# Attention of a two-layer hybrid block: where the second maximum, the second copy and the spread of the inverse sums stand in each pair of heads

## The reference

```python
def softmax_attend(q, k, v, sink):
    s = jnp.einsum('bqgrd,bkgd->bgrqk', q, k).astype(jnp.float32) * (q.shape[-1] ** -0.5)
    if sink is None:
        p = jax.nn.softmax(s, axis=-1)
    else:
        ...
        p = jax.nn.softmax(jnp.concatenate([sk, s], axis=-1), axis=-1)[..., 1:]
    return jnp.einsum('bgrqk,bkgd->bqgrd', p.astype(v.dtype), v)
...
outs.append(blocked_attend(q, jnp.concatenate([k, kc], axis=1), jnp.concatenate([v, vc], axis=1)))
```

## Time and profile before

| | |
|---|---|
| time, median of 3 runs (lowest, highest) | 2471.43 us (2469.43, 2474.56) |
| the profiled execution | 2481.41 us, span 2479.6 us |
| TensorE busy | 2265.1 us, 91% of the span |
| VectorE, ScalarE, GpSimd busy | 986.8, 678.8, 767.7 us (40%, 27%, 31%) |
| mean granted clock of TensorE | 0.946 of full |
| chain that ended last | PE 79%, DVE 12%, ACT 5% |

### The profile page before, as it was taken

How to read it: one execution, slowest core, us unless ns; L and a number is a source line. 1 busy time by engine, 2 the same in 40 slices (tenths; PEclk the granted TensorE clock), 3 DMA queues, 4 the chain that set the end, 5 groups by cost and what they waited for, 6 DMA issues and landing times.

```text
span 2479.6 us, 46004 instructions
## 1 busy us (share of the span) xinstructions
PE 2265.1 (91%) x19396; PEld 1817.8 (73%) x19396; DVE 986.8 (40%) x1477; ACT 678.8 (27%) x1181; POOL 767.7 (31%) x546
## 2 busy tenths in 40 slices
PE   5999888889989799999999899988888988999997
PEld 3888565558868488888888668846657866788886
DVE  3000555554670741414232330055556664632443
ACT  3001355641321320211111221135562222221221
POOL 2332243003213123232232244124303214444443
PEclk9999999977999899999999989899987999999998
DMA  6122000030011212212113222200030013232331
GB/s 251 54 65 108 35 1 0 6 119 3 4 53 51 94 60 65 62 59 68 59 59 134 74 80 98 79 34 1 0 117 9 4 55 125 89 98 93 94 101 59
DMA packets 45404, 162.42 MB, mean 66 GB/s; under 512 B 5504, under 2 KB 5504, under 8 KB 45024
## 3 DMA queue, kind: packets, MB, share of 16 engines
q1 hardware_dynamic: 44480, 157.89, 19.0%
q0 software_dynamic: 800, 2.69, 0.3%
HBM read 158.46 MB, written 2.10 MB: 65 GB/s over the span
## 4 chain that ended last, share of the span: by engine, by line
PE 79%; DVE 12%; ACT 5%; issue 2%; POOL 1%; DMA 0%; SPq 0%; POOLq 0%; DVEq 0%; ACTq 0%
PE ps L1364 76%; PE ps L1639 2%; DVE part_h L1014 1%; DVE small L1117 1%; DVE hT L1007 1%; DVE xT L1032 1%; DVE flat L1348 1%; ACT flat L772 1%; DVE ps L1114 1%; DVE flat L1030 1%; ACT flat L754 1%; POOL flat L527 1%; PE ps L1901 0%; DVE flat L1097 0%; ACT flat L704 0%
## 5 line engine op out<-in xcount | busy, mean ns | idle before, releaser
L1364 PE MATMUL ps<-part_hi,wparts 128*128 128x512 f32 (+1 forms) x3072 | 815.0, 353 | 28.1 <-DVE part_h L1014 10.0
L1364 PEld LDWEIGHTS ps<-part_hi,wparts 128*128 128x128 f32 x3072 | 544.9, 191 | 117.0 <-DVE part_h L1014 15.5
L508 POOL TENSOR_TENSOR wparts<-flat,wparts 128x1024 fp32r<-128x1024 f32 x184 | 447.5, 2432 | 535.1 <-ACT wparts L930 529.3
L1364 PE MATMUL ps<-flat 64*64 64x32 f32 (+8 forms) x8812 | 497.8, 266 | 68.5 <-ACT flat L772 30.3
L1364 PEld LDWEIGHTS ps<-flat 64*64 64x64 f32 (+4 forms) x8812 | 385.0, 148 | 166.7 <-issue 75.1
L1364 PE MATMUL ps<-part_h,wparts 128*128 128x512 f32 (+1 forms) x1344 | 473.8, 353 | 0.0
L1364 PE MATMUL ps<-part_mlp,wparts 128*128 128x512 f32 (+1 forms) x1536 | 417.5, 359 | 14.6 <-DVE part_h L1014 9.9
L1364 PE MATMUL ps<-part_lo,wparts 128*128 128x512 f32 x960 | 341.8, 356 | 0.0
L1364 PEld LDWEIGHTS ps<-part_mlp,wparts 128*128 128x128 f32 x1536 | 275.5, 191 | 61.9 <-DVE part_h L1014 11.6
L930 ACT ACTIVATE wparts<-flat 128x1024 fp32r<-128x1024 f32 x112 | 118.8, 1061 | 704.2 <-PE ps L1364 704.2
L1364 PEld LDWEIGHTS ps<-part_h,wparts 128*128 128x128 f32 x1344 | 257.5, 192 | 32.2 <-issue 0.2
(11 more groups left out here) (201 smaller groups left out, 1994.8 us busy)
## 6 DMA issues: line engine op xcount, KB each, us to landing
flat<-w_dram SPq DMA_DIRECT2D x128, 512.0 KB, 3.6
flat<-wmod_dram SPq DMA_DIRECT2D x88, 512.0 KB, 5.4
flat<-win_dram SPq DMA_DIRECT2D x40, 512.0 KB, 3.6
flat<-wout_dram SPq DMA_DIRECT2D x16, 512.0 KB, 3.7
hT<-wmod_dram SPq DMA_DIRECT2D x8, 512.0 KB, 7.7
xT<-xT_dram SPq DMA_DIRECT2D x8, 384.0 KB, 6.5
flat<-rope_dram SPq DMA_DIRECT2D x2, 1024.0 KB, 5.6
out_dram<-xT SPq DMA_DIRECT2D x8, 256.0 KB, 2.0
```

The costliest lines, as they stand in the source:

```text
L508: pool.tensor_tensor(wlo[q % 2], src, whi[q % 2], ALU.subtract).then_inc(s_used[q], 1)
L1364: return pe.matmul(out, lhsT, rhs, start=start, stop=stop)
```

## The change

It has four parts, all inside the loop over the pairs.

1. TensorE: `turns(2p + 1)` stands before `spread_sums(p)`. The spread no longer waits for `s_on` of the last pair, and `output` waits for `s_on` of the last pair instead of `s_spre`.
2. The spread's result has a PSUM bank of its own (bank 7) instead of a quarter of the product's bank 6.
3. ScalarE: the copy to `over_sum` stands behind the second `turned`, and waits for `s_on` of the last pair as well as for `s_spr`. In passes 1 and 2 `exps(2p + 2)` stands ahead of the second `turned`.
4. VectorE: in passes 1 and 2 both maxima stand ahead of the second `turned`; in the other passes it stays between them.

```diff
-        O_AT, SPREAD_AT = 3072, 3072 + P
+        O_AT, SPREAD_AT = 3072, 3584
...
                         for p in range(6):
+
+                            def exps_of(h):
+                                exps(h % 12, at + (12 if h >= 12 else 0))
+
                             turned(2 * p)
+                            if p in (1, 2):
+                                exps_of(2 * p + 2)
+                            turned(2 * p + 1)
                             act.wait_ge(s_spr, i * 6 + (turned0 // 2 + p + 1))
+                            act.wait_ge(s_on, 1 + i * 6 + (turned0 // 2 + p))
                             nc_.activation(over_sum, ps[:, SPREAD_AT:SPREAD_AT + P], ACT.Copy).then_inc(s_spre, 1)
-                            turned(2 * p + 1)
-                            for h in (2 * p + 2, 2 * p + 3):
-                                exps(h % 12, at + (12 if h >= 12 else 0))
+                            if p not in (1, 2):
+                                exps_of(2 * p + 2)
+                            exps_of(2 * p + 3)
...
                             for h in (2 * p + 2, 2 * p + 3):
-                                if h % 2:
+                                if h % 2 and p not in (1, 2):
                                     turned(2 * p + 1)
                                 peak(h % 12, at + (12 if h >= 12 else 0), i)
+                            if p in (1, 2):
+                                turned(2 * p + 1)
                             normed(p)
...
                             pe.wait_ge(s_sum, pairs + (p + 1))
-                            pe.wait_ge(s_on, 1 + pairs + p)
                             for g in range(2):
...
                             pe.wait_ge(s_pta, 1 + done + (2 * p + 2))
                             pe.wait_ge(s_ptd, 1 + done + (2 * p + 2))
-                            pe.wait_ge(s_spre, pairs + (p + 1))
+                            pe.wait_ge(s_on, 1 + pairs + p)
...
                             scores((p + 1) % 6, at + (2 * p + 2), i + (asked + (1 if p == 5 else 0)))
+                            turns(2 * p + 1)
                             spread_sums(p)
-                            turns(2 * p + 1)
                             output(p)
```

## The result

The changed kernel takes 2457.16 us (median of 5 runs, 2455.93 to 2458.88); the kernel before, beside it, 2474.56 us (2469.43 to 2480.43). The ratio is 0.9921 with a 95% interval of 0.9898 to 0.9945: between 14 and 25 us faster. The median moved by 17.4 us, the forecast was 12.2 us, to a time of 2459.2. The profiled execution went from 2481.41 us (span 2479.6) to 2458.63 us (span 2456.8), 22.8 us.

A forecast was written before the change was run, and what follows sets the result against it. Wide blocks were taken as bound mostly by TensorE plus one hand-over with ScalarE in each pair. Wide blocks 11.2 plus narrow 1.0 made 12.2 us, off the median 2471.43: 2459.2 us, range 2453 to 2467.

The forecast's parts named there:

- The spread leaves the path: Wide pairs: spread behind the second transposes hides in the wait for ScalarE's copy; product 0.37 us earlier, 0.36 taken.
- Passes 1 and 2: Wide blocks, low-rank scores: product comes earlier though both maxima precede VectorE's copy; saved 0.33 to 0.37, 0.36 us taken.
- Passes 3 and 4: Wide blocks, window scores: product waits for VectorE's chain, which starts at the scores in both programs; saved 0.
- Wide blocks: Eight attention blocks: four of six pairs save 0.36, 1.44 us a block, 1.26 in each layer's last; 11.2 together.
- Narrow blocks: Two blocks of layer 0, ScalarE nearly full: 0.50 us saved a block, 1.0 in all; bounds -3.4 to +4.4.
- The loss in pass 4: Narrow blocks, pair 4: second transposes may not start before ScalarE's first copy; exponential at 488.47 instead of 488.19, 0.28 lost.
- the step that gave 0: Narrow blocks, pair 3: ScalarE's exponentials start where they did, so 0 is saved.
- TensorE's clock: Rival, first narrow block's half clock: fall gone saves 4.1 us more (2455), one more gives 2463; gains beyond forecast 0.06.

The follow-up runs named there:

- the pair with the matmuls: Kernel before and changed kernel, each with three unread 512-column identity matmuls behind the narrow blocks' first scores: 2473.75 and 2458.47 us.
- the changed kernel's second trace: The changed kernel timed and profiled again without edit, beside the kernel before: 2457.01 us, ratio 0.9919.
- ScalarE's part alone: Kernel before with ScalarE's copy of the sums behind its second copy and a bank of its own, spread left in place: 2482.52 us, ratio 1.0014.
- TensorE's part alone: Kernel before with the spread behind the second transposes and its own bank, ScalarE's copy of the sums left in front: 2478.85 us, ratio 1.0014.
- the kernel before with its three matmuls: Kernel before plus three unread 512-column identity matmuls behind the narrow blocks' first scores: 2473.75 us, ratio 0.9964.

## Why the prediction was right, and where it was off

*Direction, size and range were right*, and so was the mechanism. That the time came out 2.0 us from the forecast is in part luck. The forecast was taken off the median of three runs, 2471.43 us, which is close to what the kernel before takes at its better clock (2472.9), where the changed kernel always was. Off the medians measured later (2474.56 to 2482.87) the same 12.2 us would have given 2462 to 2471 us, partly outside the range. Read by its own steps:

- **The spread leaves the path (0.37 a pass).** Right in passes 0 and 5 of the wide blocks. Idle time in front of the product fell from 0.69 to 0.32, and the spread issued twice fits in the same gap. What makes it free is the wait for ScalarE's copy, as the prediction said.
- **It is only free together with ScalarE's move.** The prediction priced the parts together and didn't say this. Each alone gave nothing (ratio 1.0014 both times).
- **Passes 1 and 2: taken 0.36, came 0.42 and 0.43.** The step compared two possible starts of the product and took the later one by ScalarE, 0.92 + 0.64 behind the scores' end. Behind the low-rank scores ScalarE's copy started only 0.77 behind the scores' end (1689.42 to 1690.19, see pass 1 above), and then VectorE's copy is the last one. The prediction's own figure by VectorE, 1709.34 against 1709.74 before, gives 0.40. The term was 16 x 0.07 = 1 us too small.
- **Passes 3 and 4: nothing, right.** From first transposes to first transposes they take 5.85 and 5.50 us, before and after.
- **Wide blocks, 1.44 a block, measured 1.59**: over eight, with the two last ones 0.2 less, 12.3 instead of 11.2 us.
- **Narrow blocks, 0.50 a block, 1.0 in all, measured 1.3.** At a clock of 1.00 in both traces (the pair with the matmuls) the first block is 0.53 shorter, 17.77 to 17.24 us from its first transposes to those of the second block. The second is 1.06 shorter up to the work behind its last product (17.77 to 16.71 us in the first profiles), but only 0.77 up to the tanh, since the last exponential stands behind the copy of the sums there. By pass the second block came as 0.22, 0.32, 0.32, 0.19, -0.21 and 0.22, where 0.18, 0.23, 0.23, 0, -0.28 and 0.14 were taken. The first block's passes 0 and 5 gained nothing (-0.03 and -0.05), since the transposes of the next pass wait for an exponential there. The row of the wait behind pass 5, in the first profile, and the rows of pass 4 of the second block:

```profile
465.56 0.41 PE L1649 MATMUL ps<-kf,flat 128*128 128x128 f32 x2 [0.30 <-ACT flat L754]
...
477.50 0.26 ACT L772 ACTIVATE flat<-ps 128x128 f32<-128x128 f32 x1
...
477.86 0.41 PE L1649 MATMUL ps<-kf,flat 128*128 128x128 f32 x2 [0.20 <-issue]
...
478.31 0.28 ACT L772 ACTIVATE flat<-ps 128x128 f32<-128x128 f32 x1 [0.55 <-PE ps L1649]
```

  The loss in pass 4 was foretold, and for this reason: ScalarE's first copy ends at 477.76, the second transposes start behind it at 477.86, the second copy is at 478.31, and both exponentials come later. The other terms were mis-sized by up to 0.1. In pass 3 the step that gave 0 was wrong by 0.19. ScalarE's exponentials did start where they did (2.03 us into the pass, 2.02 before), but the next transposes had not waited for them: they followed the product, which now comes 0.21 sooner.
- **TensorE's clock was a rival for one fall more or less, 4.1 us. It was more than that.** Passes 0 to 2 of the narrow blocks after, as the earlier trace rows:

```profile
446.20:456.60 10.40, 10.03 (x60) 6.58 (x60) 4.90 (x17) 5.85 (x24) 0.00 (x0) 0.67 0.00 1
465.56:473.68 8.12, 7.40 (x60) 4.82 (x60) 4.86 (x18) 5.85 (x25) 0.00 (x0) 1.00 0.00 0
```

  10.40 and 8.12 us instead of 13.05 and 8.98: the first block lost 2.3 us to the clock instead of 4.1. But filling the wait takes 9 us (5 to 13) off the kernel before, and nothing that could be measured off the changed one. So of the 17 to 21 us between the medians 14 to 15 are the order (12.2 forecast), and the rest is clock that the kernel before loses in more of its executions: its mean granted clock is under 0.949 in 48 of 73, that of the changed kernel in none of 13.
- **Behind the attention.** The first two profiles differ by 22.8 us, of which the attention has 15.7. The rest lies almost wholly between layer 0's tanh and layer 1's first exponential (1166.9 and 1159.9 us). From 525 to 605 us there the granted clock was 0.67 in both traces of before, and 0.79 and 0.81 in those of the changed kernel. The row of the changed kernel's second trace:

```profile
525.00:605.00 80.00, 65.14 (x1577) 58.84 (x1580) 49.76 (x81) 25.08 (x45) 24.72 (x29) 0.81 0.09 29
```

  ScalarE's part alone, TensorE's part alone and the kernel before with its three matmuls, which don't have the shorter attention, had 0.76, 0.79 and 0.77 there. So the better clock there doesn't need the shorter attention. Whether the kernel before has the poor one in most executions stays open: the runs give a mean clock, and none by stage.

The rule of the Trainium skill that was cited (TensorE: Matmul & The Clock Gate, What's actually happening) says that idle time drops the array to half rate and that the place varies from run to run. The profiles agree with the first half so far: in the narrow blocks no fall in four profiles with the wait filled, six falls in nine without. Of the second half they show that with the same wait of 1.35 to 1.36 us the fall came or stayed away, and lasted from 3 to 20 us; it began about 1 us behind the end of that wait each time (453.5 and 452.30 us in the first profile of before).

## What to carry to other kernels

Small work that stands in front of a step which another engine answers can go behind it for nothing, up to the length of the answer; but every engine in that exchange has to move with it, or the wait only changes its place. Before an order is tuned by 0.1 us a pass, look where the trace's clock falls: filling one wait of 1.4 us was worth half as much as this change in the old kernel. And where two kernels differ in how often they fall, compare them with the fall taken out of both, or by runs of the same mean clock; two profiles alone overstated this change by almost 8 us.

## What the runs showed of the hardware

- A wait of TensorE of 1.4 us between two short pieces of work was followed by 3 to 20 us of half clock in six of nine profiles. With three matmuls of 512 columns in it there was no such fall in four, and the times of the kernel before went from a scatter of 22 us to one of 5 us.
- Transposes behind matmuls with 96 rows started 0.22 after their weights began to load (1689.12 and 1689.34, rows of pass 1), while behind those with 64 rows both start together (1683.02, rows of pass 0). So the transposes of the low-rank passes came earlier than the price taken from pass 0 had them.
- An exponential pushed back by a 128-wide copy comes 0.16 later, not the copy's 0.27: in pass 0 ScalarE started it at 1684.58, 0.11 before the end of the copy.
